# Attention scores of two heads on halves of TensorE's rows, and value products of two heads on halves of its columns

## What is computed

```
x = rglru_layer(x)                  # gated linear recurrence, stage A
k, v = split(rmsnorm(x) @ w_kv)     # 2 key/value heads of 64
x = swa_layer(x, k, v)              # 16 query heads, causal window of 128, ALiBi, a sink per head
# second block
y_a = windowed_gqa(q_a, k_a, v_a)   # 8 query heads, 2 key/value heads, window +-128, a sink per head
y_b = neighborhood_attn(q_b, k_b, v_b)  # 8 heads with keys of their own, on an 8 x 64 grid
x = x + (gates * projections of y_a and y_b) @ w_out
x = x + square(relu(rmsnorm(x) @ w_up)) @ w_down
return rmsnorm(x)
```

## Time and profile before

| | |
|---|---|
| median of 3 runs | 1233.96 us (1233.89 to 1235.59) |
| the profiled execution | 1234.33 us, its span 1232.5 us |
| granted TensorE clock, mean | 0.991 of 2.4 GHz |
| TensorE matmul busy | 1203.5 us, 98% of the span |
| VectorE, ScalarE, GpSimd busy | 643.3, 524.1, 167.8 us |

### The profile page before, as it was taken

One profiled execution on the slowest core, in us unless ns is written; L12 is line 12 of the kernel. 1 busy time (PEld: TensorE's weight loads), 2 busy tenths in 40 slices (PEclk: granted clock), 3 DMA queues, 4 the chain that ended last, 5 costly groups with the idle time before them and its releaser, 6 DMA issues.

```text
span 1232.5 us, 14352 instructions
## 1 busy us (share of the span) xinstructions
PE 1203.5 (98%) x5318; PEld 945.0 (77%) x5318; DVE 643.3 (52%) x1083; ACT 524.1 (43%) x905; POOL 167.8 (14%) x215
## 2 busy tenths in 40 slices
PE   8999989999999999999999999999999999999995
PEld 5777767787776778787887777887788888888884
DVE  6787877743557665455444444546444232444221
ACT  6657746542555544233434343325433121433222
POOL 1022113220213212222111110003000000000011
PEclk9999998999999999999999999999999999999997
DMA  5322222432111123311222212232223323223211
GB/s 208 104 86 86 86 86 69 131 103 69 35 35 52 35 69 102 97 58 52 69 71 76 86 60 86 86 102 88 101 86 102 100 89 99 90 86 103 86 52 69
DMA packets 29878, 103.08 MB, mean 84 GB/s; under 512 B 3312, under 2 KB 3568, under 8 KB 29808
## 3 DMA queue, kind: packets, MB, share of 16 engines
q1 hardware_dynamic: 29376, 101.37, 25.3%
q10 hardware_dynamic: 432, 0.79, 0.2%
HBM read 100.05 MB, written 2.10 MB: 83 GB/s over the span
## 4 chain that ended last, share of the span: by engine, by line
PE 91%; DVE 4%; ACT 3%; issue 1%; DMA 1%; POOL 0%; SPq 0%; DVEq 0%; ACTq 0%; POOLq 0%
PE ps L665 26%; PE ps L667 26%; PE ps L666 25%; PE ps L804 2%; PE ps L828 2%; PE ps L771 2%; PE ps L831 1%; PE ps L779 1%; PE ps L837 1%; PE ps L792 1%; DVE cc L1277 1%; ACT wh L868 1%; PE ps L719 1%; DMA xt<-xT 1%; PE ps L737 1%
## 5 line engine op out<-in xcount | busy, mean ns | idle before, releaser
L665 PE MATMUL ps<-xgh,wh 128*128 128x512 f32 x848 | 374.4, 442 | 3.4 <-DVE wl L1170 2.9
L667 PE MATMUL ps<-xgh,wl 128*128 128x512 f32 x848 | 336.1, 396 | 0.0
L666 PE MATMUL ps<-xgl,wh 128*128 128x512 f32 x848 | 336.0, 396 | 0.0
L1170 DVE TENSOR_TENSOR wl<-raw,wh 128x1024 fp32r<-128x1024 f32 x180 | 230.2, 1281 | 154.9 <-ACT wh L868 154.8
L868 ACT ACTIVATE wh<-raw 128x1024 fp32r<-128x1024 f32 x180 | 188.3, 1048 | 134.3 <-PE ps L667 134.3
L665 PEld LDWEIGHTS ps<-xgh,wh 128*128 128x128 f32 x848 | 159.7, 188 | 48.3 <-issue 14.7
L666 PEld LDWEIGHTS ps<-xgl,wh 128*128 128x128 f32 x848 | 159.8, 188 | 40.6 <-issue 6.9
L667 PEld LDWEIGHTS ps<-xgh,wl 128*128 128x128 f32 x848 | 159.3, 188 | 37.9
L1047 ACT ACTIVATE Pt<-Pt,stat 128x256 f32<-128x256 f32 (+2 forms) x128 | 64.9, 507 | 140.9 <-DVE stat L1380 55.9
L1660 POOL TENSOR_SCALAR Pt<-Pt,stat 128x256 f32<-128x256 f32 (+2 forms) x128 | 71.1, 568 | 338.8 <-DVE stat L1412 241.9
L667 PE MATMUL ps<-fh,wl 128*128 128x512 f32 x256 | 102.1, 399 | 0.0
(11 more groups left out here) (231 smaller groups left out, 1683.1 us busy)
## 6 DMA issues: line engine op xcount, KB each, us to landing
raw<-wst SPq DMA_DIRECT2D x180, 512.0 KB, 3.5
bst<-nbias SPq DMA_DIRECT2D x8, 256.0 KB, 2.6
xt<-xT SPq DMA_DIRECT2D x3, 512.0 KB, 8.0
outT<-ot SPq DMA_DIRECT2D x6, 256.0 KB, 3.0
raw<-wst SPq DMA_DIRECT2D x2, 256.0 KB, 4.0
outT<-ot ACTq DMA_DIRECT2D x2, 256.0 KB, 2.7
cstt<-cst SPq DMA_DIRECT2D x1, 448.0 KB, 5.7
selt<-sel SPq DMA_DIRECT2D x1, 320.0 KB, 4.2
```

The costliest lines, as they stand in the source:

```text
L665: e.matmul(o, high, a, start=(k == 0), stop=False)
L666: e.matmul(o, high, b, start=False, stop=False)
L667: e.matmul(o, low, a, start=False, stop=stop).then_inc(tile_done, 1)
L1170: e.tensor_tensor(wl_t[:, u % NHL, :], raw_t[:, u % NRAW, :], f32(wh_t[:, u % NHL, :]), ALU.subtract).then_inc(lo_done, 1)
```

## The change

The heads' order in the jobs changes so that a job holds two heads of one pair and two columns of them, not four heads of one `p`. For each pair a score of `lo` is issued on rows 0 to 63 and right behind it one of `hi` on rows 64 to 127, into banks 3 and 4. The keys no longer have zeros beside them. The value products write 64 PSUM partitions each, in turn those of `lo` and of `hi`, with values that are no longer padded. The zero fills and the waits for them go, the copy of the values is one instruction instead of two, and four bias tiles are held in place of two.

```diff
-        ke = [[sb(f"ke{g}{p}", [128, S], F, ph)[:, :] for p in range(2)] for g in range(2)]
-        V1 = sb("V1", [128, 1088], F, ph)
+        ke = [sb(f"ke{g}", [128, S], F, ph)[:, :] for g in range(2)]
+        V1 = sb("V1", [128, NBLK, 128], F, ph)
...
-        bst = [sb(f"bst{i}", [128, 2, 256], F, qk) for i in range(2)]
+        bst = [sb(f"bst{i}", [128, 2, 256], F, qk) for i in range(4)]
...
             def scores(kind):
                 for m in range(*SETS[kind][:2]):
                     job = jobs[m]
-                    for i in range(4):
+                    for i in (0, 2):
                         yield step_at["score", m, i]
                         x = 4 * m + i
-                        q.wait_ge(bias_done, x - 1)
-                        o = bank[SB[x % 2]]
-                        if kind == "s":
-                            e.matmul(o[:, 0:w], q1[:, 4 * g + i, blk(n)], ke[g][p][:, keys(job)], start=True,
-                                     stop=True).then_inc(score_done, 1)
...
+                        q.wait_ge(bias_done, x)
+                        a = 2 * job["half"] + i // 2
+                        for p, r in ((0, lo), (1, hi)):
+                            o = bank[SB[p]]
+                            if kind == "s":
+                                own, seen = q1[r, 4 * g + a, blk(job["n"])], ke[g][r, keys(job)]
...
+                            e.matmul(o[:, 0:128 * job["nk"]], own, seen, start=True, stop=True).then_inc(score_done, 1)
...
-                        if kind == "s":
-                            g = job["g"]
-                            done = e.matmul(bank[PV], padded(V1, job["k0"] + kb, g, p), src, start=first and p == 0, stop=final and p == 1)
...
+                        if kind == "n":
+                            for i in range(2):
+                                a = 2 * half + i
+                                for p, r in ((0, lo), (1, hi)):
+                                    h = 2 * job["c"] + p
+                                    done = e.matmul(grid_block(bank[PV][r, :], a), Vb[:, key_block(a, kb), 64 * h:64 * h + 64],
+                                                    src[:, blk(2 * i + p)], start=first and i == 0, stop=final and i == 1)
+                        else:
+                            v = V1 if kind == "s" else Va
+                            g = job["g"]
+                            for p, r in ((0, lo), (1, hi)):
+                                done = e.matmul(bank[PV][r, 256 * half:256 * half + 256], v[:, job["k0"] + kb, 64 * g:64 * g + 64],
+                                                src.rearrange("p (c h t) -> p c h t", c=2, h=2)[:, :, p, :], start=first, stop=final)
...
             def zeros():
-                for g in range(2):
-                    for p in range(2):
-                        q.wait_ge(zero_done, 2 * g + p)
-                        e.memset(ke[g][p][64 * (1 - p):64 * (1 - p) + 64, :], 0.0).then_inc(zero_done, 1)
```

More of the change, by code:

```diff
@@ L399, in build @@
                 k0 = max(0, n - 1)
-                for p in range(2):
-                    jobs.append(dict(kind="s", g=g, n=n, p=p, k0=k0, nk=n + 1 - k0))
+                for half in range(2):
+                    jobs.append(dict(kind="s", g=g, n=n, half=half, k0=k0, nk=n + 1 - k0))
         for n in range(NBLK):
             k0, k1 = max(0, n - 1), min(NBLK, n + 2)
[L404 to L407, removed]
+            for half in range(2):
+                jobs.append(dict(kind="w", g=half, n=n, half=half, k0=k0, nk=k1 - k0))
+        for c in range(4):
+            for half in range(2):
+                jobs.append(dict(kind="n", c=c, half=half, k0=0, nk=2))
         for m, job in enumerate(jobs):
@@ L412, in build, with head @@
         SETS = {"s": (0, 16, A_END + 62.0, 0.655), "w": (16, 24, B_END + 50.0, 1.22), "n": (24, 32, B_END + 145.0, 1.6)}
+        def head(job, i):
+            return {"s": 8 * job.get("g", 0) + 4 * job["half"] + i, "w": 4 * job["half"] + i, "n": 2 * job.get("c", 0) + i % 2}[job["kind"]]
         def plan_steps(kind):
@@ L553, in biases @@
                 for h in range(8):
-                    yield end["z", 7] if h < 2 else step_at["score", 24 + h - 2, 3] + 1.0
-                    if h >= 2:
-                        q.wait_ge(bias_done, 4 * (24 + h - 2) + 4)
+                    last_use = 24 + 2 * (h // 2 - 2) + 1
+                    yield end["z", 7] if h < 4 else step_at["score", last_use, 3] + 1.0
+                    if h >= 4:
+                        q.wait_ge(bias_done, 4 * last_use + 4)
                     q.wait_ge(tile_done, B_END)
-                    e.dma_start(bst[h % 2][:, :, :], nbias[h]).then_inc(bias_in[h % 2], 16)
+                    e.dma_start(bst[h % 4][:, :, :], nbias[h]).then_inc(bias_in[h % 4], 16)
             def stores():
@@ new lines, in scores @@
+                        q.wait_ge(bias_done, x)
[4 more added lines that the diff above has]
+                                g = job["g"]
+                                q.wait_ge(qn_done, 5 + 4 * g)
+                                q.wait_ge(ke_done, 4)
+                                own, seen = q1[r, 4 * g + a, blk(job["n"])], ke[g][r, keys(job)]
+                            elif kind == "w":
+                                q.wait_ge(ev_done, ev_no(("z", 3)))
+                                q.wait_ge(ka_done, 4)
+                                own, seen = qa[r, a, blk(job["n"])], kea[r, job["g"], keys(job)]
+                            else:
+                                c = job["c"]
+                                q.wait_ge(ev_done, ev_no(("z", 10 + c)))
+                                q.wait_ge(qb_done, c + 1)
+                                q.wait_ge(ev_done, ev_no(("z", 6 + c)))
+                                own = qb[r, c, blk(a)]
+                                if a < 3:
+                                    seen = kb_t[r, c, 128 * a:128 * a + 256]
+                                else:
+                                    seen = kb_t[r, c, :].rearrange("p (b t) -> p b t", b=4)[:, 0:4:3, :]
+                            e.matmul(o[:, 0:128 * job["nk"]], own, seen, start=True, stop=True).then_inc(score_done, 1)
@@ L809, in prods @@
                     job = jobs[m]
-                    p = job["p"]
-                    r = (lo, hi)[p]
+                    half = job["half"]
                     for kb in range(job["nk"]):
@@ L1377, in biases @@
                         if kind == "s":
-                            h = 8 * job["g"] + 2 * i + job["p"]
+                            h = head(job, i)
                             bias = D1 if job["n"] else D1[:, 128:256]
```

131 lines of the change are left out of this document (32 added, 99 removed).

## The result

The changed kernel takes 1220.03 us in the median of 4 runs (1218.51 to 1220.71), the kernel before 1234.78 in its runs beside them (1233.89 to 1235.72). The ratio is 0.9881, with a 95% interval of 0.9867 to 0.9896: 1.2% faster. I had forecast 1244.4, 0.8% slower. The time is that of the rival *the passes of both heads interleave fully* (1218.7), to which I had given a chance of 0.11. The profiled execution took 1220.71 us, against 1234.33 before.

The account below looks back on a forecast made before the run. TensorE's column streaming and matmul changes were taken as the bound. Its work +11.0 us, new waits +1.0 and old waits -1.5 gave +10.5; 1234.33 + 10.5 - 0.4 = 1244.4 us, range 1238 to 1251.

Parts of the forecast that it names:

- the passes of both heads interleave fully: Rival for TensorE's `f32` pairs: two steps a pair, 25.7 us less than forecast, 1218.7 us; chance 0.11.
- three steps in place of four: Lone `f32` pair on TensorE: one pass time saved, 0.213 us at 256 columns, as starts follow program order.
- The sign of being wrong that I had named: In TensorE's records of a pair: both heads' first passes starting together would show the forecast wrong.
- TensorE's own sum: TensorE's work in scores +11.3, products +0.5, shared crossings -0.8: +11.0 us at three steps a pair.
- Crossings, 0.39 and 0.34: Switching TensorE's array into divided mode and back costs 0.39 us a run on rows, 0.34 on columns.
- Column halves overlap: Value products on TensorE's two column halves run at the same time; rival without overlap 1260 us, chance 0.13.
- The `n` blocks paid already: Value products of `n`: 16 runs already paid for division, so five steps for eight save 5.3 us.
- The waits: TensorE waiting for VectorE's bias step at scores: +1 us for new waits, -1.5 for old ones.
- the old ones: TensorE's existing 3.4 us of waits for VectorE's bias step in `s`: part goes, taken as -1.5 us.
- Zero fills, value copy, bias tiles: Work on GpSimd, ScalarE and SyncE's queue that goes with the change: costs or gives nothing on the path.
- break-even, 1.8 steps for a score of 256 columns: Score pair on TensorE: saving must pass 0.39 / 0.213 = 1.8 steps to pay for its run's crossings.

Follow-up runs that it names:

- run 2: Changed kernel with both scores of a pair on the lower 64 rows, upper heads' scores left out: 1245.29 us in one run.
- Run 1: Changed kernel with the four value products of an `n` block ordered lower, lower, upper, upper, not lower, upper, lower, upper: 1220.38 us.
- Runs 3 and 4: Changed kernel with scores as before (128 rows, padded keys), 1224.45 us; changed kernel with `s` and `w` products as before (padded values), 1225.83 us.
- runs 8 and 9: Changed kernel, job's products in one run: 8 also groups `s`/`n` score pairs, products directly at later scores, 1199.87 us; 9 places only `s` products later, 1211.67 us.

## Why the prediction was wrong

**The step that failed.** "I take starts to follow the program: the second pass of `lo` waits for the first, which holds the same rows; the first of `hi` starts with it", and from it three steps in place of four. The chain shows 0.825 us for a lone score pair, two steps and the crossings. The sign of being wrong that I had named is there too: both heads' first passes start 6 ns apart (run 2). Run 1 shows that a half does not wait for its place in the program even with four passes of the other half ahead; run 2 shows that without separate halves the two steps come back. The evidence for in-order starts was that the records of one instruction stand side by side. But in the kernel before no `f32` matmul stood next to one on another half, so those rows could not speak on it. The one place that had both halves had one pass each and did not tell the cases apart. I had listed the case, and given it 0.11 on no row against it; two cases that no row tells apart should have had chances of the same order.

**The terms.** At two steps TensorE's own sum is 11.0 - 25.7 = -14.7 us; the profiled executions differ by -13.6. So step lengths, counts and crossings were right together to about 1 us, and the passes of a pair are the one term of that sum that was mis-sized.

- *Crossings, 0.39 and 0.34*: right, in the chain of the changed kernel and in run 2, where the way back kept its 0.43. The Trainium skill's rule that a change of the tiling mode drains TensorE (TensorEngine Tiling (Array Packing), Key Properties) agrees with them.
- *Column halves overlap*: right; the forecast had it, with no row for it, so that part was luck. An `s` block takes two steps of 0.213 beside its crossings, where four had been.
- *The `n` blocks paid already*: right, and they are the largest part of the gain. Four steps of 0.11 in each of 16 blocks are 7.0 us, of the 14.7. The other products give 20.5 - 16.0 = 4.5 us and the scores 27.3 - 25.0 = 2.3, with 0.8 for shared crossings. Runs 3 and 4 measured 4.4 us for the scores and 5.8 for the `s` and `w` products, each with its shared crossings.
- *The waits*: wrong in sign. I had +1.0 and -1.5, and the sum leaves about +1.1 for them. The matmuls' waits for the bias step rose from 0.9 to 2.3 us in `s` and from nothing to 1.4 in `w`, which is +2.8 where +1 was said, and the old ones didn't go. They were to go because TensorE would be slower, and it became faster; no run parts the two. Smaller waits fell: TensorE's idle time in all (span less busy time) rose from 29.0 to 31.0 us, while its busy time fell by 15.6, and the two make the 13.6.
- *Zero fills, value copy, bias tiles*: nothing on the path, as said. The bias tiles took 4.6 us to land in the median where they had taken 2.6, and no engine's wait for them shows.

By my own break-even, 1.8 steps for a score of 256 columns, the sign of the whole change hung on one step in a pair. With such a narrow margin the chances of the two cases decide the sign of the forecast, and they had nothing behind them.

The rule of the Trainium skill on the theoretical speedup (TensorEngine Tiling (Array Packing), Theoretical Speedup: up to 2x) is borne out for the steps themselves here, 0.43 in place of 0.86. For the lone score pair of 256 columns with its crossings it comes to 0.825 against 0.86; over the whole program the steps saved come to 54.8 us and the crossings of the 111 new runs to 41.0, and that is why this change gained 1.2% and not more.

## What to carry to other kernels

Two small `f32` matmuls on separate row halves or column halves of TensorE take the time of one, beside the crossings. The order in the program didn't matter where it was tried, on column halves. Each run of them between full-size matmuls costs 0.34 to 0.39 us beside, so a single pair of 256 columns hardly pays and runs must be made long: grouping, with the products placed late enough for their inputs, gave 20 us here where the division itself had given 15. When matmuls are grouped, look at what the later members of the run wait for, since the whole run now waits for its last input, and a wait of some 2 us can cost clock on top.

## What the runs showed of the hardware

- An `f32` matmul of two passes does not hold up a later one on the other half: eight passes of 128 columns took four steps of 0.11 us both as lower, upper, lower, upper and as lower, lower, upper, upper (0.59 us with the entry, both times). On row halves the first passes of both matmuls start 6 ns apart, then both second ones.
- The two column halves take different moving data, 128 rows each, at the same time at full step: two `f32` matmuls of 256 columns, four passes, in 0.58 us with the entry, two steps of 0.213 and 0.15 (`s` products of the changed kernel).
- The weight loads of both halves overlap as well: four of 64 rows within 0.30 us, one alone 0.18 to 0.19.
- In three runs the granted clock fell to its lower level right behind a wait of TensorE of 1.7 to 2.1 us in the `s` stage: 0.83 over 10 us, 1.7 us lost each time. Not every such wait did it: runs 8 and 9 have one of 1.7 us each and a clock of 1.00 from 300 to 450 us.
